# Low parts of the context half of four norms, formed on GpSimd instead of VectorE

## What is computed

```python
def rms_norm(x, g):
    y = xf * lax.rsqrt(jnp.mean(xf * xf, axis=-1, keepdims=True) + NORM_EPS)
    return (y * g).astype(x.dtype)

def ada_pre(h, g, shift, scale):
    return rms_norm(h, g) * (1.0 + scale) + shift

for l in range(DEPTH):
    h_lat = h_lat + 0.5 * m_lat[2] * swiglu(ada_pre(h_lat, norm_g[l, 0], m_lat[0], m_lat[1]), ...)
    h_ctx = h_ctx + 0.5 * m_ctx[2] * swiglu(ada_pre(h_ctx, norm_g[l, 0], m_ctx[0], m_ctx[1]), ...)
    u_lat = ada_pre(h_lat, norm_g[l, 1], m_lat[3], m_lat[4])
    u_ctx = ada_pre(h_ctx, norm_g[l, 1], m_ctx[3], m_ctx[4])
    ...
```

## Time and profile before

| | before |
|---|---|
| median of 3 runs | 2063.23 us |
| range of the runs | 2055.83 to 2064.85 us |
| the profiled execution's own time | 2065.93 us |
| its span in the profile | 2064.2 us |
| mean granted TensorE clock | 0.984 |
| TensorE busy | 2001.7 us, 97% |
| VectorE busy | 1217.4 us, 59% |
| ScalarE busy | 650.6 us, 32% |
| GpSimd busy | 85.8 us, 4% |

### The profile page before, as it was taken

How to read it: one execution, slowest core, us unless ns; L and a number is a source line. 1 busy time by engine, 2 the same in 40 slices (tenths; PEclk the granted TensorE clock), 3 DMA queues, 4 the chain that set the end, 5 groups by cost and what they waited for, 6 DMA issues and landing times.

```text
span 2064.2 us, 25228 instructions
## 1 busy us (share of the span) xinstructions
PE 2001.7 (97%) x9676; PEld 1597.2 (77%) x9676; DVE 1217.4 (59%) x1638; ACT 650.6 (32%) x662; POOL 85.8 (4%) x157
## 2 busy tenths in 40 slices
PE   7999999999989999999999999999999997899999
PEld 3588888877867677888888688888877775499998
DVE  4777676567557757767754967233373356664445
ACT  4622222233222123222223322222243353444343
POOL 0000110000000000001100000000000002000000
PEclk8999999999999999999999999999999997999999
DMA  9155555422220014555543355222322123044553
GB/s 338 73 202 189 197 195 182 135 100 83 100 102 0 33 42 153 194 182 203 194 150 125 107 191 192 100 102 99 115 77 76 62 82 129 4 143 151 185 181 115
DMA packets 48321, 272.56 MB, mean 132 GB/s; under 512 B 5380, under 2 KB 6020, under 8 KB 24840
## 3 DMA queue, kind: packets, MB, share of 16 engines
q1 hardware_dynamic: 28536, 195.22, 26.7%
q0 software_dynamic: 19728, 76.55, 11.2%
HBM read 270.70 MB, written 1.05 MB: 132 GB/s over the span
## 4 chain that ended last, share of the span: by engine, by line
PE 89%; DVE 6%; ACT 2%; DMA 1%; issue 1%; DVEq 0%; ACTq 0%; SPq 0%
PE ps L1354 25%; PE ps L1355 25%; PE ps L1356 25%; PE ps L1628 3%; PE ps L1638 2%; PE ps L1347 1%; DVE tn L855 1%; PE ps L1718 1%; DVE act_lo L841 1%; PE ps L1797 1%; DMA w3aug<-w3aug_dram 1%; DVE w_lo L759 1%; PE ps L1681 1%; ACT w_hi L397 1%; PE ps L1552 1%
## 5 line engine op out<-in xcount | busy, mean ns | idle before, releaser
L1354 PE MATMUL ps<-act_hi,w_hi 128*128 128x512 f32 (+1 forms) x2728 | 986.9, 362 | 20.7 <-DVE w_lo L759 12.7
L1355 PE MATMUL ps<-act_lo,w_hi 128*128 128x512 f32 (+1 forms) x2728 | 981.2, 360 | 0.0
L1356 PE MATMUL ps<-act_hi,w_lo 128*128 128x512 f32 (+1 forms) x2728 | 981.1, 360 | 0.0
L759 DVE TENSOR_TENSOR w_lo<-w_raw,w_hi 128x2048 fp32r<-128x2048 f32 x172 | 394.1, 2291 | 491.0 <-ACT w_hi L397 491.0
L1354 PEld LDWEIGHTS ps<-act_hi,w_hi 128*128 128x128 f32 x2728 | 517.7, 190 | 110.2 <-DVE w_lo L759 15.0
L1356 PEld LDWEIGHTS ps<-act_hi,w_lo 128*128 128x128 f32 x2728 | 517.8, 190 | 76.0
L1355 PEld LDWEIGHTS ps<-act_lo,w_hi 128*128 128x128 f32 x2728 | 517.7, 190 | 75.2 <-issue 0.2
L397 ACT ACTIVATE w_hi<-w_raw 128x2048 fp32r<-128x2048 f32 x172 | 329.2, 1914 | 625.1 <-PE ps L1356 625.1
L781 DVE SCALAR_TENSOR_TENSOR ada_prod<-ada_w,cond_bc 128x1024 f32<-128x1024 f32 x128 | 156.1, 1220 | 1.0 <-DMA ada_w<-ada_rows_dram 1.0
L781 DVE SCALAR_TENSOR_TENSOR ada_w<-ada_w,cond_bc 128x1024 f32<-128x1024 f32 x128 | 156.3, 1221 | 0.0
L437 ACT ACTIVATE silu_g<-ps 128x1024 f32<-128x1024 f32 (+1 forms) x44 | 40.5, 920 | 307.3 <-PE ps L1356 307.3
(11 more groups left out here) (205 smaller groups left out, 1092.6 us busy)
## 6 DMA issues: line engine op xcount, KB each, us to landing
w_raw<-w_stream_dram SPq DMA_DIRECT2D x172, 1024.0 KB, 4.7
ada_w<-ada_rows_dram POOLq DMA_DIRECT2D x128, 512.0 KB, 3.7
ada_raw<-ada_stream_dram POOLq DMA_DIRECT2D x4, 1024.0 KB, 19.1
ada_in<-ada_stream_dram POOLq DMA_DIRECT2D x4, 1024.0 KB, 24.4
bd<-bd_dram SPq DMA_DIRECT2D x4, 768.0 KB, 6.2
edecay<-log_decay_dram SPq DMA_DIRECT2D x4, 512.0 KB, 21.7
h<-tokens_dram SPq DMA_DIRECT2D x1, 2048.0 KB, 26.2
wg<-wg_dram SPq DMA_DIRECT2D x3, 512.0 KB, 5.2
```

The source lines that it names most:

```text
L759: dve.tensor_tensor(w_lo[:, g % 2, :], w_raw[:, g % 2, :], w_hi[:, g % 2, :].bitcast(F32), ALU.subtract).then_inc(w_lo_done, 1)
L1354: pe.matmul(out, wh, xh, start=start, stop=False)
L1355: pe.matmul(out, wh, xl, start=False, stop=False)
L1356: return pe.matmul(out, wl, xh, start=False, stop=stop)
```

## The change

For norms 1 to 4, VectorE's function `lo` leaves out the context half and forms the latent half alone. GpSimd forms the context half in two instructions a tile: it adds the shift to the context half of `tn` in place (TENSOR_SCALAR), waits for that by a semaphore of its own (`uctx_sum`), and subtracts `act_hi` into `act_lo` (TENSOR_TENSOR), which signals `uctx_ready`. VectorE's `tn(k)` for `k >= 4` waits for `uctx_ready` of tile `k - 4` as well, and TensorE waits for it at each tile. The one loop of row loads becomes three, with the norms between them: tiles up to 53, norms 1 and 2, tiles 54 to 105, norm 3, tiles 106 to 127, norm 4.

```diff
-            with pool.Fori(1, ADA_TILES // 2) as q:
-                for s in range(2):
-                    pool.wait_ge(adaw_used, 4 * q - 2 + 2 * s)
-                    pool.dma_start(ada_w[:, s],
-                                   dram["ada_rows"][bass.ds(2 * q + s, 1)].rearrange("a p k -> (a p) k")
-                                   ).then_inc(adaw_loaded[s], 16)
-
+            def row_tiles(first, last):
+
+                with pool.Fori(0, (last - first) // 2) as i:
+                    for s in range(2):
+                        pool.wait_ge(adaw_used, 2 * first - 2 + 2 * s + 4 * i)
+                        pool.dma_start(ada_w[:, s],
+                                       dram["ada_rows"][bass.ds(first + s + 2 * i, 1)].rearrange("a p k -> (a p) k")
+                                       ).then_inc(adaw_loaded[s], 16)
+
+            def context_lo(n):
+
+                for k in range(KT):
+                    pool.wait_ge(uhi_ready, 8 * n + k + 1)
+                    pool.tensor_scalar(tn[:, k % 4, 0:CTX], tn[:, k % 4, 0:CTX], mods[:, 24 * n + k, 0:1], None,
+                                       ALU.add).then_inc(uctx_sum, 1)
+                    pool.wait_ge(uctx_sum, 8 * (n - 1) + k + 1)
+                    pool.tensor_tensor(act_lo[:, k, 0:CTX], tn[:, k % 4, 0:CTX], act_hi[:, k, 0:CTX].bitcast(F32),
+                                       ALU.subtract).then_inc(uctx_ready, 1)
+
+            row_tiles(2, 54)
+            context_lo(1)
+            context_lo(2)
+            row_tiles(54, 106)
+            context_lo(3)
+            row_tiles(106, ADA_TILES)
+            context_lo(4)
...
-                        if c.start >= cols.start:
+                        if c.start >= cols.start and (n in (0, 5) or c.start):
                             last = dve.scalar_tensor_tensor(act_lo[:, k, c], tn[:, k % 4, c],
...
                     if k >= 4:
                         dve.wait_ge(u_ready, k - 3 + 8 * n)
+                        if 1 <= n <= 4:
+                            dve.wait_ge(uctx_ready, k - 3 + 8 * (n - 1))
...
                         pe.wait_ge(u_ready, 8 * norm_n + k + 1)
+                        if 1 <= norm_n <= 4:
+                            pe.wait_ge(uctx_ready, 8 * (norm_n - 1) + k + 1)
                         for t in range(2):
                             mm = pe.matmul(ps[:, bank + t, cols], wh[:, k, c[t]], act_lo[:, k, cols],
                                            start=False, stop=False)
                         continue
                     if norm_n is not None:
                         pe.wait_ge(u_ready, 8 * norm_n + k + 1)
+                        if 1 <= norm_n <= 4:
+                            pe.wait_ge(uctx_ready, 8 * (norm_n - 1) + k + 1)
```

More of the change, by code:

```diff
@@ L213, in build @@
         tn_ready, uhi_ready, u_ready = sem("tn_ready"), sem("uhi_ready"), sem("u_ready")
+        uctx_sum, uctx_ready = sem("uctx_sum"), sem("uctx_ready")
         sq_added, in_free = sem("sq_added"), sem("in_free")
```

## The result

The changed kernel took 2084.32 us (median of 4 runs, 2072.87 to 2086.48) against 2059.53 us of the kernel before beside it: ratio 1.0116, 95% interval 1.0083 to 1.0148. So the change makes the kernel 0.9 to 1.2% slower, where I had forecast no change that can be told. (The ratios given in this text come from the single runs and differ from the quotient of two medians by up to 0.2%.)

The account below looks back on a forecast made before the run. TensorE was taken to bound the kernel, with VectorE setting the norms' tile pace. Saving 0.2 us a norm, 1 us in all, gave 2065 for the profiled execution and a median of 2062; forecast's own range 2058 to 2066, 8-in-10 range 2055 to 2077.

Parts of the forecast that it names:

- Where TensorE's time goes: Whole kernel: TensorE busy 97% of the span; gains only where it idles, in the four norms; cutting the row loads costs nothing.
- What GpSimd adds: GpSimd in norms 1 to 4: two instructions a tile, TENSOR_SCALAR 0.58 us and TENSOR_TENSOR 0.74, together 1.32 us (bounds 1.13 and 1.53).
- item (2): End of a norm: `w_lo` due at 471.0, held up 0 to 0.5 us by GpSimd's last instruction, ending at 473.4 to 473.8.
- What the two engines do to each other: Norm tiles: contention with `act_lo` makes GpSimd's tile 1.57 us and VectorE's 1.52 us; `tn` takes no wait.
- third rival: Norms: the engines hardly meet or TENSOR_SCALAR is cheap; 4 to 9 us faster in all, around 2057; chance 0.13.
- clearly slower: Norms: GpSimd at 2.0 us a tile, or `tn` held up too; 4.9 us a norm, 20 in all, 2083; chance 0.17.
- The sum for a norm: Norm 1: second block starts at 473.3 to 473.8 against 473.76; 0.2 us less a norm, 1 us in all.
- item (1): Norm 1: GpSimd starts at 459.1, ends its eighth tile at 471.7 at 1.57 us each; TensorE's last tile ends at 473.1.
- first slower rival: GpSimd's last tile falls behind `w_lo` if its tile needs over about 1.6 us; 9 us in all, 2072; chance 0.25.

Follow-up runs that it names:

- e1: The kernel before with only the row-load loop cut in three, VectorE forming both halves again; ratio 0.9998 to the kernel before.
- e2: The changed kernel with GpSimd's TENSOR_SCALAR replaced by a TENSOR_TENSOR adding the shift as broadcast operand; ratio 0.9997 to the kernel before.
- e4: The changed kernel with VectorE waiting for GpSimd's last tile before it forms `w_lo` in norms 1 to 4; ratio 1.0057 to the kernel before.
- e3: The changed kernel without GpSimd's first instruction, so the shift is left out of the context low parts; ratio 0.9974 to the kernel before.
- e8: The changed kernel with the shift added by ScalarE, GpSimd keeping only the difference, and `w_hi` moved ahead as in e7; ratio 0.9979 to the kernel before.
- e5: The changed kernel with the edits of e2 and e4 together; ratio 1.0001 to the kernel before.
- e9: e8 with `w_lo` made to wait for GpSimd's last tile, the edit of e4; 2052.67 us against 2064.07 of the kernel before, ratio 0.9947.
- e7: The kernel before with ScalarE forming `w_hi` of the second block ahead of its eight `act_hi` in norms 1 to 4; ratio 0.9981.
- e10: The changed kernel unaltered, run once more on the same chip as e9; ratio 1.0089 to the kernel before.

## Why the prediction was wrong, point by point

**Where TensorE's time goes.** Right. The stretches of the norms carry the whole difference (23.1 us of 20 to 25), and the row loads nothing (e1). One reading was off: the window of norm 4 in the earlier trace rows reaches 0.9 us into the second block, and the stretch there is 16.6 us like the others.

**"What GpSimd adds": the step that failed.** I priced the sum at 0.58 us, by VectorE's ratio of one input to two, and let 0.79 us, the two-input price, be the upper bound, "one operand less to read". It takes 0.92 us undisturbed (0.84 with a constant), 0.34 us a tile more than I had in the sum. The bound was no bound: here the form that reads less is the dearer one. The two-input price stood in the trace; the other was a guess by analogy, and with a second error (item (2) of the sum, below) the guess decided the sign. The difference was priced right, 0.72 to 0.74 us also with its output in the rounded format.
The Trainium skill, page "GPSIMD Engine Reference", section "Engine selection", has one-input work on GpSimd near line rate and two-input work about half as fast as VectorE's. This case's trace does not agree for this instruction: it took 0.92 us against 0.72 us for two inputs, and more than the 0.55 us of VectorE's one-input form on twice the elements. The measurement decides.

**"What the two engines do to each other".** The mechanism was right, and so, nearly, was its size for GpSimd. In e2 the sum costs 0.61 us by itself, close to the 0.58 of the prediction, and `act_lo` holds it up by another 0.19 (I had 0.25); the tile is 1.57 us in three norms, the very number of the prediction, and 1.45 in the fourth. In the changed kernel 1.97 us is likewise about 0.25 us above the 1.72 us that its tiles take in e4 with VectorE waiting. For VectorE the size depends on where the two fall: e2 has 1.57 us a tile where I had 1.52, but the changed kernel's first tiles came 1.2 to 1.3 us apart. This mattered in another way than I thought: a faster VectorE reached the wait for GpSimd's tile `k - 4` earlier, and that wait, which I had called met below 2.1 us a tile, held the last two `tn` at 1.97.
That `tn` itself does not contend the runs now show: 0.86 us a pair beside GpSimd in e3 and e8, as alone. This agrees with the Trainium skill, page "SBUF — State Buffer", section "Who interferes with whom", by which a VectorE instruction with at most one SBUF input does not contend with GpSimd. (The prediction calls a held-up `tn` the third rival's case; it is the second's, "clearly slower".)

**"The sum for a norm".** With 1.57 us a tile and `w_lo` (2.35 us) behind GpSimd it gives 14.5 + 2.35 = 16.9 us from the first `tn`; e5 measured 16.9 in norm 1 and 16.1 where the tile was 1.45 us. So the arithmetic was sound. Two of its inputs were not. First the price: at 1.97 us a tile item (1) becomes 457.1 + 8 x 1.97 = 472.9, in the times of the changed kernel's trace. Then item (2), where GpSimd was to come first and `w_lo` to lose up to 0.5 us, turned round: `w_lo` came first, and GpSimd lost 2.05 us to it (2.97 against 0.92) and ended at 474.5. In norm 3 it lost 2.9 us more to what follows. This second error does not hang on the price alone: in three norms of e2, at the very pace of the prediction, `w_lo` came first too.

**The rivals.** What came was the one that I called clearly slower, with 0.17: 2.0 us a tile, `w_lo` in between, 4.9 us a norm, 2083 us. The runs gave 1.97 us, 2.05 us for `w_lo`, 4.2 to 5.4 us a norm and 8.4 in norm 3, 2084 us. Its numbers hold, its reason doesn't: neither rounding nor a held-up `tn` made GpSimd slow, and that its 2.0 us a tile, taken from the masks, met the 1.97 is luck. The first slower rival named the same place, and its point of decision, about 1.6 us a tile, is borne out by e2: at 1.57 us GpSimd met `w_lo`, at 1.45 it did not. A GpSimd instruction that came just behind `w_lo` took 2.97, 2.87 and 2.76 us, which is nearly the 2.29 us of `w_lo` and its own time: it waited for all of it. These rows agree with the Trainium skill, page "SBUF — State Buffer", section "SBUF: two separate sides", which calls the shared port an exclusive lock for the whole instruction.

**Not foreseen at all.** The 1.2 GHz level that TensorE had behind its wait in norms 1 and 3, 1.2 us in norm 1, and the gates' weights in norm 3, which I had not looked at because they stand behind the norm.

## What to carry to other kernels

Price an instruction that the trace does not show on its engine by more than analogy with another engine, and keep a bound only if something forbids the far side; where the forecast's sign hangs on it, that one price is the first thing to measure. When work is handed from VectorE to GpSimd, list every VectorE instruction with two SBUF inputs that can meet it, the long ones behind the handed-over piece above all, and put a wait in their way or a third engine's step between, as e9 does. And look for idle time on the engine that ends the tail: moving `w_hi` up, off the end of a norm, won 0.2% (e7).

## What the runs showed that I had not expected

- On GpSimd, for 128x256 float32: TENSOR_TENSOR 0.72 us, with a broadcast second operand 0.61 us (0.80 beside VectorE's `act_lo`), TENSOR_SCALAR with a constant 0.84 us, with a pointer 0.92 us.
- A GpSimd instruction that starts 0.01 us behind a 2.29 us VectorE instruction with two SBUF inputs takes 2.87 us; where it had started 0.67 us ahead, and the two overlapped by 0.07 us, neither paid (e2).
- The stretches of the same program agree to 0.02 us in two executions from different batches, while its total moves by 8 us from run to run (e10); in the twelve traces norm 0 begins 5 to 10 us later where TensorE waits for one load near 40 us and has the 1.2 GHz level around it.
